# Relative bias fetched key-reversed, and TensorE sharing the modulation column sums, in a one-core decoder block

## The reference

```python
cond = jax.nn.silu(c)
mod = cond @ ada_w[l] + ada_b[l]                      # 1024 -> 6 x 1024
sh1, sc1, gt1, sh2, sc2, gt2 = jnp.split(mod[:, None, :], 6, axis=-1)
h = rms_norm(x, pre_g1[l]) * (1.0 + sc1) + sh1
...
proj = h @ w_in                                       # q, k, v, z_u, z_v, two gates
...
lg = (jnp.einsum('bhqd,bhkd->bhqk', qc, k_own).astype(jnp.float32) * scale
      + rb[:, t5_bucket(rel)])                        # rel = query position - key position
```

## Time and profile before

| | us |
|---|---|
| median of 3 runs | 1598.76 (1597.06 to 1599.52) |
| the profiled execution | 1599.17, its span 1597.2 |
| TensorE busy | 1501.3 (94%) |
| VectorE busy | 1337.7 (84%) |
| GpSimd busy | 804.4 (50%) |
| ScalarE busy | 668.0 (42%) |

### The profile page before, as it was taken

The page is one execution under the profiler, slowest core; times in us unless marked ns, Lnnn a source line. Parts: engine busy times, 40 slices in busy tenths (PEclk is TensorE's granted clock), DMA queues, the critical chain, the costliest instruction groups (busy, mean ns, idle before and its releaser), DMA issues.

```text
span 1597.2 us, 25315 instructions
## 1 busy us (share of the span) xinstructions
PE 1501.3 (94%) x7879; PEld 1279.6 (80%) x7879; DVE 1337.7 (84%) x2628; ACT 668.0 (42%) x1213; POOL 804.4 (50%) x757
## 2 busy tenths in 40 slices
PE   4999999999998958699999999999999999999996
PEld 3678776685777747588999999999999999999995
DVE  5777634452899889889999999999999999999998
ACT  4332445412127754444444444434444444444443
POOL 1000000001009978677766766767667667667662
PEclk8999999999999969999999999999999999999998
DMA  9975211232011437999999999999999999999994
GB/s 347 391 255 199 93 53 53 89 127 104 1 54 71 114 76 222 212 364 405 406 405 397 404 379 389 405 361 400 399 370 400 390 374 406 382 376 406 376 390 163
DMA packets 212878, 447.58 MB, mean 280 GB/s; under 512 B 80235, under 2 KB 98947, under 8 KB 212556
## 3 DMA queue, kind: packets, MB, share of 16 engines
q1 hardware_dynamic: 156620, 242.08, 42.9%
q0 software_dynamic: 56192, 204.66, 32.7%
HBM read 423.78 MB, written 22.32 MB: 279 GB/s over the span
## 4 chain that ended last, share of the span: by engine, by line
PE 79%; DVE 9%; issue 4%; DMA 3%; POOL 2%; ACT 2%; SPq 0%; POOLq 0%; DVEq 0%; ACTq 0%
PE bank L908 14%; PE bank L1114 8%; PE bank L1115 8%; PE bank L1113 8%; PE bank L1137 7%; PE bank L1135 7%; PE bank L1136 7%; PE bank L1127 3%; PE bank L1128 3%; PE bank L1062 3%; PE bank L845 2%; PE bank L1074 2%; DMA w_scratch<-staged 2%; PE bank L1011 2%; POOL hot L780 1%
## 5 line engine op out<-in xcount | busy, mean ns | idle before, releaser
L1113 PE MATMUL bank<-h_hi,u_hi 128*128 128x320 f32 x960 | 297.4, 310 | 8.7 <-DVE u_lo L1952 8.7
L753 POOL DMA_INDIRECT v_rows<-v_exp,small x192 | 256.7, 1337 | 91.2 <-POOL small L749 51.8
L753 POOL DMA_INDIRECT u_rows<-u_exp,small x192 | 254.9, 1328 | 93.1 <-POOL small L749 52.0
L1114 PE MATMUL bank<-h_lo,u_hi 128*128 128x320 f32 x960 | 298.0, 310 | 0.0
L1115 PE MATMUL bank<-h_hi,u_lo 128*128 128x320 f32 x960 | 298.0, 310 | 0.0
L1464 ACT ACTIVATE v_hi<-v_raw 128x1024 fp32r<-128x1024 f32 x128 | 135.4, 1058 | 170.1 <-PE bank L1137 170.1
L1137 PE MATMUL bank<-v_hi,g_both 128*128 128x512 f32 x512 | 203.9, 398 | 0.0
L1135 PE MATMUL bank<-v_hi,g_both 128*128 128x512 f32 x512 | 202.7, 396 | 0.0
L1136 PE MATMUL bank<-v_lo,g_both 128*128 128x512 f32 x512 | 202.7, 396 | 0.0
L1113 PEld LDWEIGHTS bank<-h_hi,u_hi 128*128 128x128 f32 x960 | 181.3, 189 | 13.8 <-issue 8.9
L1114 PEld LDWEIGHTS bank<-h_lo,u_hi 128*128 128x128 f32 x960 | 181.2, 189 | 6.2
(11 more groups left out here) (250 smaller groups left out, 2973.2 us busy)
## 6 DMA issues: line engine op xcount, KB each, us to landing
v_raw<-v_exp SPq DMA_DIRECT2D x128, 512.0 KB, 7.9
u_raw<-u_by_key SPq DMA_DIRECT2D x120, 512.0 KB, 5.9
ada_blk<-ada_w SPq DMA_DIRECT2D x22, 1024.0 KB, 10.1
ring<-w_in SPq DMA_DIRECT2D x18, 1024.0 KB, 5.2
w_scratch<-staged SPq DMA_DIRECT2D x4, 4096.0 KB, 24.4
w_row<-w_scratch SPq DMA_DIRECT2D x128, 128.0 KB, 9.2
xr<-x SPq DMA_DIRECT2D x8, 512.0 KB, 6.0
ring<-w_branch SPq DMA_DIRECT2D x4, 1024.0 KB, 5.0
```

What stands on the lines that cost most here:

```text
L753: pool.indirect_dma_start(out=rows[s], out_offset=None, in_=table, in_offset=bass.IndirectOffsetOnAxis(ap=ix[:, s:s + 1], axis=0))\
L1113: pe.matmul(o, u_hi[:, r, k], h2_hi[:, k], start=(k == 0), stop=False)
L1114: pe.matmul(o, u_hi[:, r, k], h2_lo[:, k], start=False, stop=False)
```

## The change

Two things. First, the one-hot matrix `hot` is laid out for the other direction (`bucket_onehot`), so that the fetch gives each partition its query with the keys reversed. It lands in `bias` itself, and `biased` reads it with a step of -1. The antidiagonal matrix, its load, the eight turning products and the eight copies on ScalarE are gone. The fetch is issued later: `bias` lies where `nat` lay, so GpSimd waits for the transposes and for VectorE's fifth sum (that of block 5).

Second, the column sums of blocks 1, 2 and 3. For blocks 2 and 3 (`BY_HALVES`) VectorE sums row tiles 4 to 7 only; tiles 0 to 3 are multiplied on TensorE, `column_products`, with the weights of `ada_w` as the loaded operand and `scol` as the moving column, into columns 0 to 3 of the bank, and `columns` puts VectorE's part beside it into columns 4 to 7; `column` adds both. Block 1 is done by TensorE alone, all eight row tiles, and VectorE's `chunks(1)` is gone. `summed(n)` counts VectorE's sums without it. The buffers of blocks 1, 2 and 3 are now read by TensorE too, so SP waits for those products ahead of the next load.

```diff
-    n = (S - 1) - np.arange(2 * S)
+    n = np.arange(2 * S) - (P - 1)
...
-BIAS_FIRST = [("bt", h) for h in range(4)] + [("col", 1), ("col", 3)] + [("bt", h) for h in range(4, H)]
+LATE_COLS = [("col", 1), ("col", 3)]
+BY_HALVES = (2, 3)
+
+
+def summed(n):
+
+    return n + 1 - sum(ADA_ORDER[m] == 1 for m in range(n + 1))
...
                 if turn_of:
-                    sp.wait_ge(chunks_summed, max(m for m in range(n) if ada_place(m)[0] == r) + 1)
+                    before = max(m for m in range(n) if ada_place(m)[0] == r)
+                    sp.wait_ge(chunks_summed, summed(before))
+                    if ADA_ORDER[before] in BY_HALVES:
+                        multiplied(sp, ("col", ADA_ORDER[before]))
...
-            sp.dma_start(anti, anti_in).then_inc(ident_landed, 16)
             load_ada(1)
             load_ada(3)
             load(BLOCKS[0], 1)
             load_ada(4)
-            sp.wait_ge(chunks_summed, 3)
+            multiplied(sp, ("col", 1))
             load(BLOCKS[1], 0)
...
-            pool.wait_ge(chunks_summed, 2)
-
-            pool.dma_start(flipped, bass.AP(bias_dram.tensor, 0, [[1, P], [2 * S, H], [1, S]]))\
-                .then_inc(bias_in, 16)
+            multiplied(pool, *group("xT"))
+            pool.wait_ge(chunks_summed, summed(5))
+            pool.dma_start(bias, bass.AP(bias_dram.tensor, 0, [[1, P], [2 * S, H], [1, S]])).then_inc(bias_in, 16)
...
+            def column_products(b, halves):
 
                 n = ADA_ORDER.index(b)
                 pe.wait_ge(cond_ready, 1)
-                pe.wait_ge(chunks_summed, n + 1)
+                for half in halves:
+                    w = ada_landed(pe, b, half)
                 o = start("col", b)
+                rows = range(4 * halves[0], 4 * halves[-1] + 4)
                 for j in range(4):
-                    last = pe.matmul(o[:, j:j + 1], sums[:, n % 2, j * P:(j + 1) * P], ones[:, 0:1], start=True, stop=True)
+                    for k in rows:
+                        last = pe.matmul(o[:, j:j + 1], w[:, k, j * P:(j + 1) * P], scol[:, k:k + 1],
+                                         start=(k == rows[0]), stop=(k == rows[-1]))
+                return last
...
             columns(0)
+            column_products(2, (0,))
             columns(2)
             pair(0)
+            full(column_products(1, (0, 1)), "col", 1)
+            column_products(3, (0,))
+            columns(3)
             pair(1)
-            pe.wait_ge(bias_in, 16)
-            pe.wait_ge(ident_landed, 32)
-            for job in BIAS_FIRST:
-                if job[0] == "bt":
-                    product(job, [(anti, flipped[:, job[1], :])])
-                else:
-                    columns(job[1])
...
-            bias_rows(range(6))
             high(2)
-            bias_rows(range(6, H))
...
-                w = ada_landed(dve, b, 0)
-                ins = dve.tensor_scalar(s, w[:, 0, :], scol[:, 0:1], None, ALU.mult)
-                for k in range(1, KD):
+                first = KD // 2 if b in BY_HALVES else 0
+                w = ada_landed(dve, b, first // 4)
+                ins = dve.tensor_scalar(s, w[:, first, :], scol[:, first:first + 1], None, ALU.mult)
+                for k in range(first + 1, KD):
...
                     link(dve.tensor_tensor(scale_col[:, at_b], o[:, 0:4], ada_b_col[:, KD:2 * KD][:, at_b], ALU.add))
+                    link(dve.tensor_tensor(scale_col[:, at_b], o[:, 4:8], scale_col[:, at_b], ALU.add))
...
             low(1)
-            chunks(1)
             chunks(3)
...
-                    link(dve.tensor_tensor_reduce(out=prob(h, i), in0=o[:, 0:w], in1=bias[:, h, S - w:S], scale=1.0,
+                    link(dve.tensor_tensor_reduce(out=prob(h, i), in0=o[:, 0:w], in1=bias[:, h, w - 1::-1], scale=1.0,
...
-            stored(dve, *group("bt"))
+            dve.wait_ge(bias_in, 16)
             biased(0)
```

More of the change, by code:

```diff
@@ L170 @@
 place(begun(range(0, 2)), LOW)
-place(BIAS_FIRST, HIGH)
+place(LATE_COLS, HIGH)
 for _p in range(2, 20):
@@ L265, in build @@
         kT = at("kT", 143.5, [P, NT, S])
-        anti = at("anti", 143.5, [P, P])
         va = at("va", 151.5, [P, NT, S])
@@ L277, in build @@
         gg = at("gg", 191.5, [P, NT, D])
-        flipped = at("flipped", 159.5, [P, H, S])
         h2_own = at("h2_own", 20, [P, D])
@@ L869, in _ @@
                     transposes(("xT", t, f), [nat[:, t, (4 * f + k) * P:(4 * f + k + 1) * P] for k in range(4)])
+            def column_products(b, halves):
+                n = ADA_ORDER.index(b)
+                pe.wait_ge(cond_ready, 1)
+                for half in halves:
+                    w = ada_landed(pe, b, half)
+                o = start("col", b)
+                rows = range(4 * halves[0], 4 * halves[-1] + 4)
+                for j in range(4):
+                    for k in rows:
+                        last = pe.matmul(o[:, j:j + 1], w[:, k, j * P:(j + 1) * P], scol[:, k:k + 1],
+                                         start=(k == rows[0]), stop=(k == rows[-1]))
+                return last
             def columns(b):
@@ L874, in columns @@
                 pe.wait_ge(cond_ready, 1)
-                pe.wait_ge(chunks_summed, n + 1)
-                o = start("col", b)
+                pe.wait_ge(chunks_summed, summed(n))
+                o = bank("col", b) if b in BY_HALVES else start("col", b)
+                at_b = 4 if b in BY_HALVES else 0
                 for j in range(4):
-                    last = pe.matmul(o[:, j:j + 1], sums[:, n % 2, j * P:(j + 1) * P], ones[:, 0:1], start=True, stop=True)
+                    last = pe.matmul(o[:, at_b + j:at_b + j + 1], sums[:, n % 2, j * P:(j + 1) * P], ones[:, 0:1],
+                                     start=True, stop=True)
                 full(last, "col", b)
@@ L1207, in rows_high @@
                 act.activation(hT_hi[:, 2 * q:2 * q + 2], xnT[:, 2 * q:2 * q + 2], ACT.Copy).then_inc(h_hi_done, 1)
[L1209 to L1212, removed]
             def out_of_banks(b):
```

## The result

| | before | with the change |
|---|---|---|
| median, us | 1599.18 | 1605.47 |
| range | 1597.06 to 1600.44, 6 runs | 1603.83 to 1606.42, 6 runs |
| ratio, 95% interval | | 1.0038 (1.0027 to 1.0048) |
| the profiled execution, its span | 1599.17, 1597.2 | 1604.32, 1602.4 |
| TensorE busy | 1501.3 (94%) | 1518.6 (95%) |

A forecast was written before the change was run, and what follows sets the result against it. TensorE, busy 94.33 of 94.60 us from 81 to 176 us, was taken as the bound, so pair(2)'s start and clock decide; 1598.8 - 4.0 = 1594.8 us, forecast's own range 1592.5 to 1596.5, stretched to 1608 for Rival 1.

The forecast's parts named there:

- the term between `pair(0)` and `pair(1)`: Between these pairs, 52 column products replace turning products, at full clock; four pairs end 3.5 to 4.5 us earlier, -4.0 taken.
- Rival 1: Clock falls under one-column products between pair(0) and pair(1): four pairs end 8.1 us later, 1606.9 us; chance 0.30.
- The first sum: Block 2's sum ahead of pair(0), halved with TensorE: -1.7 us with the clock held, -0.3 if it falls.
- The gap and the slow stretch ahead of `pair(2)`: TensorE's idle time and low clock around pair(2)'s start vanish; it starts at 56.0 and four pairs end at 77.9.
- The covers: Later bias transfer, held-back second weight block and VectorE's path to pair(4) stay hidden behind other work, costing nothing.
- The reversed read: Bias read with step -1 in the addition: put at 0, bounds 0 to 15.7 us; as a rival, slower, chance 0.04.

The follow-up runs named there:

- wide96: The changed kernel with its column products 96 columns wide instead of one, nothing else moved: 1594.15 us, ratio 0.9963 to the kernel before.
- col1_split: The changed kernel with block 1's sum back on VectorE and pair(1) cut in two, columns of 1 and 3 between its halves: 1593.27 us, ratio 0.9961.
- split_wide: col1_split with the column products 96 columns wide: 1590.58 us, ratio 0.9942 to the kernel before.
- col1_dve: The changed kernel with block 1's sum back on VectorE, columns of 1 and 3 behind pair(1): 1595.06 us, ratio 0.9973 to the kernel before.
- first_only: bias_only plus the 16 one-column products of block 2 ahead of pair(0): 1593.74 us, ratio 0.9970 to the kernel before.
- bias_only: The changed kernel with only the new bias path; VectorE sums all four blocks again, late columns behind pair(1): 1592.18 us, ratio 0.9952 to the kernel before.

## Why the prediction was wrong, step by step

**The step that failed** is the term between `pair(0)` and `pair(1)`: "52 x 0.23 = 12.0 us at the full clock, 52 x 0.46 = 23.9 at half". The forecast took the first, with 0.53, against 0.30 for the rival. Measured: 19.28 us, 7.3 more. The clock held for three microseconds of the run and then fell. With this the end of the pairs adds up: forecast 77.9, plus 1.3 for a later `pair(0)` (31.78, not 30.5), less 0.8 for a shorter one (7.27 us, not 8.05), plus 7.3 for the products and 1.9 for the slow start of `pair(1)` makes 87.6, the measured end. The row that I leaned on, 16 records between wide products at a clock of 1.00, was not a run of that kind, and the second argument (the clock was high when the sixteen products at 21.19 began) held only for those sixteen: it was lost at their end, and the `columns(2)` behind them ran at 0.46 a product (1.84 us).

**Rival 1** had the mechanism and nearly the size: +8.1, against +6.2 at the end of the pairs and +6.3 in the medians. Its products were put at 19.6 us (19.28 measured), `pair(0)` at 31.9 (31.78). The first of these is in part luck: the clock fell after 3.0 us of the run and not 4.5, and a slow product took 0.43 us (sixteen from 49.66 to 56.49) and not 0.46; the two misses partly cancel. Too dear were `pair(0)`, whose clock rose sooner and which ended at 39.05, not 40.1, and the slow beginning of `pair(1)`: put at +2.6, while 120 records in 29.27 us stand against 27.33 at the full clock (5 x 5.47), +1.9.

**The first sum**: forecast -1.7, with -0.3 as its other end. Measured: the scaled rows at 28.32 instead of 28.73, `pair(0)` at 31.78 instead of 32.18, -0.4: the other end, and nearly for the reason given with it. VectorE's half started at 22.37, not 22.0, because the last transfer landed there; the clock fell as the sixteen products ended, and `columns(2)` took 1.84 us and not 0.92. (The prediction's -0.3 doesn't follow from its own numbers: -1.7 + 1.6 is -0.1. The measured value lies near both.) With 96 columns `pair(0)` began at 30.65, -1.5, with `columns(2)` at the full clock. So the term was right in its own condition, and the condition failed. (48 columns gave 30.69: ahead of `pair(0)` they kept the clock, 3.61 us for the sixteen products, and only the longer run between the pairs lost it. What makes the two places differ, the runs don't separate.)

**The gap and the slow stretch ahead of `pair(2)`**: gone, as forecast. The end of the pairs that was built on it, 77.9, was reached at 77.97 once the clock held (wide96).

**The covers** held: the second weight block at 49.83 instead of 42.41 made nobody wait, the bias transfer landed at 94.5 us for a use at about 188, VectorE was in time for `pair(4)`, with the clock kept too (wide96, where TensorE runs without a wait from 50.60 to 77.97). `pair(4)` waited for VectorE only in col1_split and split_wide, where half of `pair(1)`, 2.7 us, no longer stands between `columns(3)` and `pair(4)`.

**The reversed read** was put at 0 out of 0 to 15.7 us: 691 against 692 ns for 512 elements. The section of the Trainium skill that was cited ("Vector Engine (DVE) Microarchitecture Reference", 5.1) gave no mode to lose, and the trace agrees.

**What the weighing should have been.** The prediction said itself that no row showed such a run, and that a product of one column moves almost nothing. Where a term is 12.0 at one clock and 23.9 at the other and no row decides, the two deserve equal weight at least; the range held the time only because the rival's case was in it.

## What to carry to other kernels

Moving small reductions to TensorE as one-column products can cost more than their own time: back to back they lost the clock here, at 100% busy, and the wide products behind them paid too. Try a wide moving operand for such products (here 96 columns came at the price of one, with the weight load busy 4.00 of 4.00 us in either case), and read a stretch by its records and its granted clock, never by its busy share. When a change has two halves, run them apart: here one was worth 7 us in the medians and the other took all of it and more. And read such a change at the end of the stage that it touches (here the end of the pairs), not at the end of the program alone.

## What the runs showed of the hardware

- f32 products with 128x128 weights and 1 or 96 moving columns take the same time at the full clock (0.116 us a record in 3.71 us for 32 of one column, 0.114 in 7.28 us for 64 of 96). With 1, 16 and 48 columns, between the pairs, the granted clock went from 1.00 to 0.50 within a run that had no pause; with 96 it stayed.
- Sixteen such products are enough. Between the pairs, 32 records took 3.46 us at the full clock, and half clock came at their end (col1_dve); ahead of `pair(0)` it came within them, at 23.5 us of products begun at 21.66 (first_only).
- One-column products hold the clock no better than a pause: it fell at 24.6 us with TensorE idle from 21.09 (bias_only), and at 24.8 with sixteen of them in that place; with 96 columns it fell at 29.6.
- The Trainium skill, "TensorE: Matmul & The Clock Gate", section "Why this matters for your kernels", ties drops within a kernel to idle gaps between bursts. Here the clock fell with TensorE busy 4.00 of 4.00 us.
- A two-source f32 operation of VectorE whose second operand has a step of -1 takes the time of one with a step of +1 (691 and 692 ns for 128x512).
